# Sample rows read from PSUM, searches in eight steps, and fourteen lookups ahead at each unit's boundary in a two-layer attention and expert-retrieval kernel

## Chip, cores and metric

The kernel runs on one core of a Trainium2 chip. The metric is the device time of one execution in microseconds, the median of the runs. Everything is float32.

## What is computed

One step of a two-layer network over 384 tokens: 128 prompt tokens and 256 sample tokens, each of width 1024. Each layer has a dense half (modulated norm, one input projection, two kinds of attention and a short convolution, output projection) and then an expert retrieval, which takes most of the time here:

```python
q = (xc @ wq).reshape(128, 8, 2, 128)                  # 8 heads, 2 halves
sc = einsum('thcd,hcnd->thcn', q, sub_keys)            # 128 keys a half
s1, i1 = top_k(sc[:, :, 0], 16); s2, i2 = top_k(sc[:, :, 1], 16)
cand = s1[..., :, None] + s2[..., None, :]             # 256 pairs a head
top_s, pos = top_k(cand, 16)
eidx = (i1 * 128 + i2 of those pairs)                  # rows of two 16384-row tables
gate = softmax(top_s)
act = gelu(einsum('thkd,td->thk', take(u_tab, eidx), xc))
out = einsum('thk,thkd->td', gate * act, take(v_tab, eidx))
```

So each token reads 8 x 16 = 128 rows of 4 KB from the first table (U) and the same rows of the second (V), in each of two layers.

## The kernel before

**Units.** The 384 tokens are three tiles of 128, one token on each of 128 partitions. Tile 0 is the prompt, tiles 1 and 2 are the samples. A tile in a layer is called `tau` (0 to 5: prompt, sample, sample, and again for layer 1). Its 128 picks per token are two units of 64, so there are 12 units; unit `u` belongs to `tau = u // 2`. A lookup is one indirect DMA issued by GpSimd (L618): it takes one pick of all 128 tokens and brings 128 rows of 1024 floats into one of the 14 slots of `ring`. Each unit needs 64 U lookups and 64 V lookups, 1536 in all.

**What is done with a row.** For a U row VectorE computes the product with the token's own row and its sum (`dot`, L1381): in place in `ring`, with `h2[:, tau % 3, :]`, both in SBUF. After 64 of them `coefficients` (L1388 to L1397) makes the unit's factors, with a tanh on ScalarE. `turn` (L861, L862) transposes factors and picks on TensorE into `ps_acc`, ScalarE copies them (`copy_turned`, L1050 and L1051, and `spread`, L1069), and GpSimd makes `v_rows` of them (`take_unit`, L596). Only then can the unit's V lookups be issued. TensorE adds V rows in quads, four lookups at a time, with 16 matmuls (`add_rows`, L875), and frees four slots together. At the end of a `tau`, `copy_sum` (L1075) and `feed` (L1405 to L1409) bring the sum into `x`.

**Searches.** `route(n)` (L1329 to L1360) does the two-stage top 16 of one head for a tile on VectorE, some 30 instructions in a row. GpSimd's `take_head` (L588) waits for its picks before the head's first U lookup. Searches are made two heads ahead, in the middle of a head's 16 products.

**Segments.** Every engine walks the same list by hand. A segment has a unit `u` whose U rows are multiplied, a unit `v` (the one before) whose V rows are added, and sometimes dense work beside it:

```python
s0, p1, s1 = (0, S_TILES), (1, P_TILES), (1, S_TILES)
return (Segment(0, None, s0), Segment(1, 0, s0, True),
        Segment(2, 1), Segment(3, 2, p1), Segment(4, 3, p1), Segment(5, 4, p1), Segment(None, 5, p1, True),
        Segment(6, None, s1), Segment(7, 6, s1, True),
        Segment(8, 7), Segment(9, 8), Segment(10, 9), Segment(11, 10), Segment(None, 11))
```

`s0` and `s1` are the sample tiles' dense half in layers 0 and 1, `p1` the prompt's in layer 1; the prompt's in layer 0 comes first, alone. Segments with nothing beside them are called plain here: (2, 1), (8, 7), (9, 8), (10, 9), (11, 10), and the last. A segment has 64 items; at each item every engine first does its share of the dense work (`side.item()`), by a fixed weight, and then VectorE does `dot(i)`, and TensorE, at each fourth item, `add_rows` of V rows i-3 to i. The order in each engine's queue is fixed.

**Order of lookups.** `lookups()` writes GpSimd's order out. In a segment with both units the first `LEAD` = 6 places are U lookups only, then U and V alternate, and the last 6 are V lookups only; so seven U lookups stand ahead of V row 0. A lookup waits until the one 14 places before it has been used (`free_slot`), by VectorE for a U row and by TensorE for a V row.

**PSUM.** It has four tensors of 1024 columns: `ps_acc` for the sums, `ps_mb`, `ps_mm` and `ps_tr` for the dense work. Attention scores (`scores`, L754) alternate between the two halves of `ps_mm`, so that score `g` waits for exponential `g - 2`; transposed probabilities (`transpose_probs`, L765) alternate between the two halves of `ps_tr`. In a B head two score maps are made: VectorE takes the maxima of both (L1231, L1232), ScalarE the exponentials (L974), VectorE mixes them.

## Time and profile before

| | |
|---|---|
| median of 3 runs | 3205.22 us (3202.32 to 3216.55) |
| profiled execution: its own time | 3236.59 us |
| profiled execution: span in the profile | 3234.8 us |
| mean granted clock of TensorE | 0.684 of full speed |
| lookups | 805.40 MB of 963.27 MB moved |
| first U lookup of the segments (0,-), (1,0), (2,1), (3,2) | 269.7, 411.8, 807.2, 1003.0 us |
| of (4,3), (5,4), first V lookup of (-,5), then (6,-), (7,6) | 1212.8, 1478.6, 1704.2, 1796.6, 1925.3 us |
| of (8,7), (9,8), (10,9), (11,10), first V lookup of (-,11) | 2316.0, 2516.4, 2717.1, 2912.7, 3125.6 us |

Times are microseconds from the start of the span unless marked ns. PE is TensorE, DVE VectorE, ACT ScalarE, POOL GpSimd. A line of the timeline gives start, duration, engine, line of the kernel, operation and operands; in brackets stands how long the engine had been idle before it and what ended that. A name of a tensor can be that of another in the same memory (`h<-...` and `scores` are views).

### The profile page before, as it was taken

To read this page: it belongs to the slowest core of one execution; us is meant where nothing else is said; L and a number is where in the kernel's file an instruction comes from. 1 tells how busy PE (TensorE), PEld (TensorE's weight loads), DVE (VectorE), ACT (ScalarE), POOL (GpSimd) and SP (SyncE) were. 2 spreads that over 40 slices of the span, in tenths; PEclk is the share of its full clock that TensorE was granted. 3 is DMA by queue.
4 is the path that set the end of the run, shared out by engine and by line. 5 is a ranking of instruction groups with operands and counts; after the bars stand their busy time and mean duration, and the time that the engine had idled before them with its cause. 6 is when DMAs were issued, how large, how long until landed. Compare 5 with 4: busy or idle time off the path is not lost.

```text
span 3234.8 us, 22432 instructions
## 1 busy us (share of the span) xinstructions
PE 1552.9 (48%) x6476; PEld 676.8 (21%) x6476; DVE 1635.3 (51%) x3970; ACT 278.2 (9%) x730; POOL 1715.8 (53%) x1601
## 2 busy tenths in 40 slices
PE   6666668567234433333445747856423222232334
PEld 2343235244001110111222225424300000000001
DVE  1406676454656555455532596543556555565420
ACT  0211013011000000010000103210100000000000
POOL 0004511355677777436665660247577777777755
PEclk9778765788557666666678875677765656665567
DMA  8668962589998999658999890379799999998988
GB/s 298 247 237 281 353 220 85 208 319 341 361 332 319 379 380 368 241 198 301 340 375 368 312 359 26 125 268 360 258 333 335 326 337 346 345 349 316 339 313 311
DMA packets 299017, 963.27 MB, mean 298 GB/s; under 512 B 28280, under 2 KB 30712, under 8 KB 298128
## 3 DMA queue, kind: packets, MB, share of 16 engines
q0 software_dynamic: 221184, 805.40, 67.9%
q1 hardware_dynamic: 77712, 156.44, 13.4%
q8 instruction: 53, 0.87, 0.1%
q14 instruction: 68, 0.56, 0.0%
HBM read 959.12 MB, written 2.62 MB: 297 GB/s over the span
## 4 chain that ended last, share of the span: by engine, by line
issue 24%; PE 22%; POOL 19%; DMA 18%; DVE 14%; another core or an unknown queue 1%; ACT 1%; POOLq 0%; SPq 0%; DVEq 0%; ACTq 0%
POOL ring L618 19%; DMA ring<-peer_v,v_rows 11%; PE ps_acc L875 7%; DVE ring L1381 4%; PE ps_mm L700 3%; PE ps_mm L754 2%; PE ps_mm L813 2%; DMA weights<-ada_w 2%; DMA ring<-peer_u,u_rows 2%; PE ps_mm L841 1%; PE ps_mb L780 1%; DMA weights<-w_in 1%; DMA weights<-peer_wq 1%; PE ps_tr L765 1%
## 5 line engine op out<-in xcount | busy, mean ns | idle before, releaser
L875 PE MATMUL ps_acc<-ring,coef_cols 128*32 128x512 f32 x3072 | 629.5, 959 | 1327.4 <-DMA ring<-peer_v,v_rows 1310.7
L1381 DVE CUSTOM_DVE_ANT_0 ring<-ring,h 128x1024 f32<-128x1024 f32 x768 | 917.2, 1224 | 636.2 <-DMA ring<-peer_u,u_rows 611.5
L618 POOL DMA_INDIRECT ring<-peer_u,u_rows x768 | 842.4, 1097 | 635.8 <-DVE dots L1381 386.3
L618 POOL DMA_INDIRECT ring<-peer_v,v_rows x768 | 839.4, 1093 | 398.0 <-issue 217.3
L875 PEld LDWEIGHTS ps_acc<-ring,coef_cols 128*32 128x32 f32 x3072 | 124.2, 148 | 1756.8 <-issue 1755.6
L700 PE MATMUL ps_mm<-weights,hT 128*128 128x512 f32 x480 | 217.3, 612 | 30.1 <-DMA weights<-w_in 25.6
L841 PE MATMUL ps_mm<-hT,weights 128*128 128x128 f32 (+1 forms) x1024 | 201.3, 355 | 26.5 <-DMA weights<-peer_wq 21.4
L841 PEld LDWEIGHTS ps_mm<-hT,weights 128*128 128x128 f32 x1024 | 171.7, 213 | 92.1 <-issue 53.0
L588 POOL TENSOR_SCALAR u_rows<-picks 128x16 uint32<-128x16 f32 x48 | 23.6, 493 | 302.7 <-DVE picks L1360 301.7
L700 PEld LDWEIGHTS ps_mm<-weights,hT 128*128 128x128 f32 x480 | 92.9, 196 | 154.6 <-issue 117.3
L1405 DVE TENSOR_TENSOR h<-h,ps_acc 128x1024 f32<-128x1024 f32 x6 | 7.3, 1222 | 197.7 <-PE ps_acc L875 197.7
L813 PE MATMUL ps_mm<-weights,hT 128*128 128x512 f32 x192 | 95.8, 657 | 9.5 <-DMA weights<-w_out 6.2
L1231 DVE TENSOR_REDUCE rowmax<-ps_mm 128x1 f32<-128x384 f32 (+1 forms) x108 | 50.0, 463 | 91.4 <-PE ps_mm L754 79.3
L661 PE MATMUL ps_acc<-weights,condT 128*32 128x512 f32 x384 | 63.9, 798 | 66.6 <-DMA weights<-ada_w 66.6
L596 POOL TENSOR_SCALAR v_rows<-turned_rows 128x64 uint32<-128x64 f32 x12 | 8.3, 696 | 162.4 <-ACT turned L1051 162.4
L754 PE MATMUL ps_mm<-h,scores 32*128 32x384 f32 (+1 forms) x144 | 81.0, 849 | 23.8 <-ACT scores L974 20.2
L1069 ACT ACTIVATE coef_cols<-turned 64x16 f32<-64x16 f32 x96 | 21.9, 228 | 798.1 <-PE ps_acc L875 545.6
L1131 DVE TENSOR_TENSOR mods<-mods,ps_acc 128x512 f32<-128x512 f32 x24 | 16.5, 686 | 130.7 <-PE ps_acc L661 126.5
L1309 DVE TENSOR_TENSOR merged<-merged,ps_mb 128x512 f32<-128x512 f32 x12 | 8.2, 687 | 129.8 <-ACT merged L1004 129.8
L1381 DVE DVE_READ_ACCUMULATOR2_ANT dots<- 128x1 f32 x768 | 63.2, 82 | 0.0
L974 ACT ACTIVATE scores<-ps_mm,negmax 128x384 f32<-128x384 f32 (+1 forms) x108 | 54.3, 507 | 64.4 <-DVE negmax L1232 64.4
L1027 ACT ACTIVATE proj<-ps_mm 128x128 f32<-128x128 f32 (+1 forms) x64 | 21.1, 330 | 447.5 <-PE ps_mm L841 254.6
(182 smaller groups left out, 1539.3 us busy)
## 6 DMA issues: line engine op xcount, KB each, us to landing
weights<-ada_w SPq DMA_DIRECT2D x24, 2048.0 KB
weights<-w_in SPq DMA_DIRECT2D x20, 2048.0 KB
weights<-peer_wq SPq DMA_DIRECT2D x16, 2048.0 KB
weights<-w_out SPq DMA_DIRECT2D x8, 2048.0 KB
ring<-peer_u,u_rows POOLq DMA_INDIRECT x768
ring<-peer_v,v_rows POOLq DMA_INDIRECT x768
weights<-peer_keys SPq DMA_DIRECT2D x4, 1024.0 KB
par<-params SPq DMA_DIRECT2D x2, 1026.0 KB, 7.0
```

Of the source, the lines that this page charges most:

```text
L618: pool.indirect_dma_start(ring[:, place % RING, :], None, src, bass.IndirectOffsetOnAxis(ap=rows, axis=0)).then_inc(row_full[place % RING] ...
L661: last = pe.matmul(ps_acc[QROWS * j:QROWS * (j + 1), n % 2 * NB:(n % 2 + 1) * NB], condT[:, k, at:at + QROWS], w[:, k, :], start=(i == 0), ...
L700: last = pe.matmul(mm(i), hT[:, k, j * P:(j + 1) * P], w[:, k, :], start=(k == 0), stop=(k == KC - 1))
L754: pe.matmul(mm(g, nk * P), q, k, start=True, stop=True, tile_position=(lo, 0)).then_inc(score_mm, 1)
L765: last = pe.transpose(tr(head)[:, s * P:(s + 1) * P], w_.probs[:, probs_slot(head), s * P:(s + 1) * P], ident)
L780: last = pe.matmul(ps_mb[:, col:col + HD], w_.probsT[:, head % 2, s * P:(s + 1) * P], v, start=(s == 0), stop=(s == nk - 1))
L813: pe.matmul(mm(i), hT[:, k, j * P:(j + 1) * P], w[:, k, :], start=(k == 0), stop=(k == KC - 1))
L841: last = pe.matmul(mm(i, nt * P), w[:, k, (i % 4) * P:(i % 4 + 1) * P], hT[:, k, 0:nt * P], start=(k == 0), stop=(k == KC - 1))
L875: last = pe.matmul(ps_acc[QROWS * k:QROWS * (k + 1), b * NB:(b + 1) * NB], coef_cols[:, i // PART % 2, at:at + QROWS], ring[:, slot("v", n ...
L974: act.activation(w_.probs[:, probs_slot(head, second), 0:nk * P], mm(g, nk * P), ACT.Exp, bias=negmax[:, u:u + 1], scale=float(HD if u < A ...
L1231: step.after(dve.tensor_reduce(rowmax[:, u:u + 1], mm(j * UNITS + u, nk * P), AXX, ALU.max))
L1381: dve.tensor_tensor_reduce(row, row, h2[:, n // (2 * UNIT) % T, :], 1.0, 0.0, ALU.mult, ALU.add, dots[:, n // UNIT % 2, n % UNIT:n % UNIT ...
```

## The change

1. In the products of sample units (2 to 5 and 8 to 11, 512 of the 768) the token's row is read from `ps_tr`. A new ScalarE step, `hold_rows`, copies the 1024 columns of `h2` there, once for each of the four sample tiles and layers, when the tile before has all its products done; VectorE waits for it before the first product.
2. `ps_tr` is therefore taken while layer 1's prompt dense work (`p1`) runs beside units 3 to 5. For that work alone (`tight`) transposes go to `ps_mm` or a half of `ps_mb`, all scores to one half of `ps_mm` (score `g` waits for exponential `g - 1`), all transposed probabilities to the other half (one buffer in place of two), and TensorE transposes a head's probabilities before it makes the next scores.
3. `route` is a generator of eight steps; from the middle of a head on, one step is done before each product. Where a search's result is needed at once, it is run through whole, as before.
4. `LEAD` is 14: fifteen U lookups stand ahead of V row 0, and 14 V lookups alone end the segment. TensorE's `add_rows` and ScalarE's `spread` come `LAG` = 8 items later in segments with a U unit, and the last eight rows are added after the items.

```diff
-LEAD = 6
+LEAD = 14
+LAG = 8
+SAMPLES = [l * T + t for l in range(DEPTH) for t in S_TILES]
+        def tight(l, tiles):
+            return l > 0 and tiles == P_TILES
+        def scores_at(l, tiles, g, n):
+            return mm(0, n) if tight(l, tiles) else mm(g, n)
+        def probs_at(l, tiles, head, n):
+            return mm(1, n) if tight(l, tiles) else tr(head, n)
+        def buffers(l, tiles):
+            return 1 if tight(l, tiles) else 2
...
+                if l and tiles == S_TILES:
+                    pe.wait_ge(u_used, l * 2 * T * UNIT)
...
-                            if g >= 2:
-                                pe.wait_ge(exp_ready, nth(l, tiles, UNITS, g - 2))
+                            if g >= buffers(l, tiles):
+                                pe.wait_ge(exp_ready, nth(l, tiles, UNITS, g - buffers(l, tiles)))
...
-                        if head + 1 < HEADS:
+                        if head + 1 < HEADS and not tight(l, tiles):
                             scores(head + 1)
                         if head >= 1:
                             transpose_probs(head - 1)
+                        if head + 1 < HEADS and tight(l, tiles):
+                            scores(head + 1)
...
+                lag = 0 if g.u is None else LAG
...
-                    if g.v is not None and i % QUADS == QUADS - 1:
-                        add_rows(g.v, i - QUADS + 1)
+                    if g.v is not None and i % QUADS == QUADS - 1 and i >= lag:
+                        add_rows(g.v, i - lag - QUADS + 1)
+                for i in range(UNIT - lag if g.v is not None else UNIT, UNIT, QUADS):
+                    add_rows(g.v, i)
...
+            def hold_rows(tau):
+                act.wait_ge(u_used, 2 * tau * UNIT)
+                act.wait_ge(ps_ready, group_nth(tau // T, S_TILES, 15, 16))
+                act.wait_ge(h_ready, nth(tau // T, S_TILES, 2, 2 * len(S_TILES) - 1))
+                act.activation(ps_tr[:], h2[:, tau % T, :], ACT.Copy).then_inc(h_held, 1)
...
                 if g.u is not None:
                     gelu_tanh(g.u)
+                    if g.u % 2 and not g.last and (g.u + 1) // 2 in SAMPLES:
+                        hold_rows((g.u + 1) // 2)
...
                 if g.last:
                     side.end()
+                    if g.u is not None:
+                        hold_rows((g.u + 1) // 2)
...
-                dve.tensor_tensor_reduce(row, row, h2[:, n // (2 * UNIT) % T, :], 1.0, 0.0, ALU.mult, ALU.add,
+                tau = n // (2 * UNIT)
+                h = h2[:, 0, :]
+                if tau in SAMPLES:
+                    h = ps_tr[:]
+                    if n % (2 * UNIT) == 0:
+                        dve.wait_ge(h_held, held(tau))
+                dve.tensor_tensor_reduce(row, row, h, 1.0, 0.0, ALU.mult, ALU.add,
...
                     if i % TOPK == TOPK // 2 and head == routed and (head % P_HEADS or head // P_HEADS % T == 2):
-                        route(routed)
+                        for _ in routing:
+                            pass
+                        routing = route(routed)
                         routed += 1
+                    next(routing, None)
```

## Rows read from the trace of the kernel before

**Rows 1.** The page: GpSimd's busy tenths and the DMA engines' in 40 slices.

```profile
POOL 0004511355677777436665660247577777777755
DMA  8668962589998999658999890379799999998988
```

**Rows 2.** Windows, one for each stage or group of stages.

```profile
core 0: us, PE busy (x) PEld busy (x) DVE busy (x) ACT busy (x) POOL busy (x), PEclk, DMA share, GB/s
807.20:1003.00 195.80, 51.27 (x232) 9.99 (x236) 118.78 (x295) 1.42 (x6) 141.85 (x134) 0.56 0.94 348
2316.00:3112.20 796.20, 223.82 (x1006) 44.02 (x1006) 445.56 (x1042) 11.60 (x46) 579.81 (x531) 0.59 0.92 336
...
1003.00:1212.80 209.80, 88.61 (x346) 26.61 (x341) 117.85 (x280) 10.53 (x24) 145.60 (x134) 0.67 0.96 361
1212.80:1478.60 265.80, 92.16 (x398) 31.28 (x394) 138.53 (x370) 24.32 (x74) 137.60 (x133) 0.62 0.75 267
1478.60:1704.20 225.60, 109.82 (x554) 50.79 (x546) 102.69 (x211) 19.23 (x54) 139.70 (x133) 0.72 0.93 349
...
411.80:807.20 395.40, 267.08 (x1072) 158.16 (x1072) 214.86 (x534) 70.52 (x176) 137.32 (x133) 0.72 0.64 231
1925.30:2316.00 390.70, 257.56 (x1024) 156.63 (x1024) 206.72 (x519) 70.19 (x176) 140.85 (x133) 0.71 0.56 200
```

**Rows 3.** GpSimd's lookups: two groups from 2316 to 3112 us, then L618 from 3126.

```profile
L618 POOL DMA_INDIRECT ring<-peer_v,v_rows x256 | 284.4, 1111 | 116.8 <-issue 74.8 <-DVE dots L1381 24.6 <-remote 11.1
L618 POOL DMA_INDIRECT ring<-peer_u,u_rows x256 | 281.6, 1100 | 88.0 <-issue 74.4 <-PE ps_acc L875 7.3 <-POOL u_rows L588 6.4
...
L618 POOL DMA_INDIRECT ring<-peer_v,v_rows x64: 932/937/1022, 3125.6 to 3214.3; - x64
```

**Rows 4.** Timeline: lookups beside products (L1381) and beside L1405.

```profile
2500.10 1.99 POOL L618 DMA_INDIRECT ring<-peer_u,u_rows  x1 [0.30 <-issue]
...
2504.68 0.94 POOL L618 DMA_INDIRECT ring<-peer_u,u_rows  x1 [0.30 <-issue]
...
2510.68 1.23 DVE L1381 CUSTOM_DVE_ANT_0 ring<-ring,h 128x1024 f32<-128x1024 f32 x1 [3.42 <-DMA ring<-peer_u,u_rows]
...
2522.16 1.22 DVE L1405 TENSOR_TENSOR h<-h,ps_acc 128x1024 f32<-128x1024 f32 x1 [8.81 <-PE ps_acc L875]
2522.70 0.94 POOL L618 DMA_INDIRECT ring<-peer_u,u_rows  x1 [0.31 <-issue]
```

**Rows 5.** GpSimd's waits: the span, then 2316 to 3112 us (total, times, longest).

```profile
POOL ring L618 <- DVE dots L1381: 459.0, 81, 19.0
...
POOL ring L618 <- PE ps_acc L875: 10.9, 15, 1.9
```

**Rows 6.** Timeline of GpSimd at boundaries between segments.

```profile
2514.26 0.94 POOL L618 DMA_INDIRECT ring<-peer_v,v_rows  x1 [0.30 <-issue]
...
2531.43 1.02 POOL L618 DMA_INDIRECT ring<-peer_v,v_rows  x1 [0.91 <-POOL v_rows L596]
...
1494.45 1.00 POOL L596 TENSOR_SCALAR v_rows<-turned_rows 128x64 uint32<-128x64 f32 x1 [7.37 <-ACT turned L1051]
...
2020.50 0.37 POOL L596 TENSOR_SCALAR v_rows<-turned_rows 128x64 uint32<-128x64 f32 x1 [55.61 <-ACT turned L1051]
...
2314.88 0.25 POOL L588 TENSOR_SCALAR u_rows<-picks 128x16 uint32<-128x16 f32 x1 [18.66 <-DVE picks L1360]
```

**Rows 7.** Timeline inside the attention of layer 1's prompt tokens.

```profile
1367.09 3.60 PE L875 MATMUL ps_acc<-ring,coef_cols 128*32 128x512 f32 x16 [11.18 <-DMA ring<-peer_v,v_rows]
...
1371.66 0.37 ACT L974 ACTIVATE scores<-ps_mm,negmax 128x128 f32<-128x128 f32 x1
...
1371.98 0.49 DVE L1329 MAX8 half_top<-scores 128x8 f32<-128x128 f32 x2
...
1372.17 0.87 PE L754 MATMUL ps_mm<-scores,h 32*128 32x128 f32 x4 [0.63 <-ACT scores L974]
...
1381.33 0.19 DVE L1360 SCALAR_TENSOR_TENSOR picks<-pair_key 128x32 f32<-128x32 f32 x1
...
1383.48 1.14 POOL L618 DMA_INDIRECT ring<-peer_u,u_rows  x1 [18.96 <-DVE dots L1381]
```

More of the change, by code:

```diff
@@ L679, in norm @@
                     for k in range(KC):
-                        last = pe.transpose(ps_tr[:, k * P:(k + 1) * P], src[:, k * P:(k + 1) * P], ident)
+                        last = pe.transpose(transposed(l, tiles)[:, k * P:(k + 1) * P], src[:, k * P:(k + 1) * P], ident)
                     last.then_inc(h_mm, 1)
@@ L799, in dense_stages @@
                     for k in range(KC):
-                        last = pe.transpose(ps_tr[:, k * P:(k + 1) * P], merged[:, k * P:(k + 1) * P], ident)
+                        last = pe.transpose(transposed(l, tiles)[:, k * P:(k + 1) * P], merged[:, k * P:(k + 1) * P], ident)
                     last.then_inc(mergedT_mm, 1)
@@ L1084, in _ @@
                     side = start_beside(of, modulate, dense_stages)
+                lag = 0 if g.u is None else LAG
                 if g.v is not None:
```

68 lines of the change are left out of this document (44 added, 24 removed).

## Prediction

> **What bounds the kernel now.** I read the page first: its busy lines, then its slices over time, to see which engine could be the limit [rows 1]. None is: GpSimd is busy 53% of the span, TensorE and VectorE no more. The DMA line is at 8 or 9 tenths in most slices and falls to 0 to 3 around two places, near 450 us and near 1970 us. So I cut the span into the kernel's own stages, by the first lookup of each unit in the timeline [rows 2]. Three kinds show. In the five plain stages, where only lookups, products and sums run, the DMA engines are busy 92 to 94% at 336 to 348 GB/s. Beside layer 1's prompt tokens it is 96%, 75%, 93%. In the two stages beside sample tokens it is 64% and 56%: there the order of the dense work sets the time, not the lookups.
>
> Next, what a lookup costs. A lookup is one GpSimd instruction and 128 rows of 4 KB, 0.524 MB. Alone it takes 0.94 us and the next follows 0.30 us behind, so 1.24 us [rows 3]. In the four plain stages from 2316 to 3112 us the 512 lookups take 1.11 and 1.10 us each, 0.17 above 0.94: 512 x 0.17 = 86 us of GpSimd time. The timeline says when: a lookup issued while products (L1381, two operands in SBUF) run back to back takes 1.99 us, it ends with a product; one that runs across L1405, the same length but with one operand in PSUM, takes 0.94 [rows 4].
>
> The last stretch has lookups of V alone and no products: 64 of them from 3125.6 to 3214.3 us, 88.7 / 63 = 1.41 us each, all of 0.94 us [rows 3]. So with GpSimd free the transfers themselves set the pace. The best mixed stage, at 1003 us, moves 361 GB/s [rows 2]; 0.524 MB at 361 GB/s is 1.45 us.
>
> Last, who makes GpSimd wait [rows 5]: over the span VectorE's products (slots of the ring not yet free), 459 us in 81 waits. In the four plain stages TensorE's additions, which hold the V slots, make it wait only 11 us.
>
> **The change part by part.**
>
> (a) *Products from PSUM.* The 512 products of units 2 to 5 and 8 to 11 read `ps_tr` in place of `h2`. By the L1405 pair they take as long and no longer hold GpSimd [rows 4]. A lookup there goes back to 1.24 us, which is under the 1.45 of the transfers, so the transfers become the limit. Now the five plain stages take 195.8 + 796.2 (four of them) = 992 us for 640 lookups, 1.55 each [rows 2].
>
> (b) *Fourteen lookups ahead.* At an even V unit the chain is: last V lookup 2514.26, sums, L1405, turn, `v_rows`, first V lookup 2531.43. That is 17.2 us [rows 6]. Seven U lookups, 8.7 us, stand in it now; the next V row comes fifteen U lookups on, 15 x 1.24 = 18.6 us, so the rest of the chain is covered, at the transfers' pace amply. What could be late next is U row 14, which needs the slot of product 0; it comes behind `feed`, whose three 1.2 us steps begin with L1405 at 2522.2 [rows 4], with the gate between them: about 2529, before the slot is wanted at 2534. The v-only tail grows from 6 to 14 lookups. VectorE has no product in it; it is busy 119 of 196 us [rows 2], so this has cover in plain stages.
>
> So a plain stage is 128 lookups at a pace r plus about 1.2 us for `take_unit`. From below r is 1.41, the V stretch; from above 1.53, which the stage at 807 does already (195.8 / 128). A second limit: the first V slot of a quad is wanted again 8 lookups after the quad's last lookup starts; that takes about 6.0 us until it is used (issued 2504.68, product at 2510.68 [rows 4]) and 3.6 us of L875 [rows 7], with TensorE's granted clock at 0.56 to 0.59 in these stages, mostly its lower level, 1.2 GHz [rows 2], 10 us with the semaphores, or 1.25 us a lookup, and 1.4 to 1.45 when a landing is 1 to 1.5 us late. I take 1.45, nearer the V stretch since its rate has been seen in a mixed stage too. 640 x 1.45 + 6 = 934: **58 us less**; the bounds give 84 and 7.
>
> The Trainium skill (DMA: Bandwidth & Descriptors, "Where 436 GB/s comes from") puts the HBM side at about 358 GB/s for one core, which would speak against any large gain: 0.524 MB / 358 = 1.46 us, an estimate, and the same five stages at 943 us, 49 less. The stage at 1003 moves 361, so the trace agrees within 1%.
>
> (c) *Searches in eight steps.* Each of VectorE's searches (L1329 to L1360) is 9.5 us without a product between, as from 1371.98 to 1381.5, and GpSimd's wait of 18.96 us ends behind it [rows 7]. Between products the steps are 1 to 3 us, and two lookups take 2.5 us, so most of a search is then under the issue of lookups. In plain stages it is in (a)'s pace. In the two sample stages and at the prompt's attention the engines wait for each other in turn; I count 5 us for each sample stage (0 to 12) and 6 for the prompt stage.
>
> (d) *Prompt attention of layer 1 in one score buffer.* This adds waits. The second map of a B head (6 of them) may only be scored after the first one's exponential: the exponential starts at 1371.66 and the score that waits for it at 1372.17, 0.5 us; the score takes up to 0.5, and two semaphores 0.4, so 1.4 us in which VectorE waits in order and the products behind it too [rows 7]. Each of 12 heads has its transpose ahead of its score, 0.4 us and the copy's signal: 12 x 0.5. Together 14 us, bounds 0 (other waits cover it; TensorE comes 11.2 us late with the quad before anyway) and 40 (each map, 18, waits 2.2 us).
>
> (e) *The stages beside layer 1's prompt.* At 1003 us the DMA engines are busy 96%: 4 us. At 1212 (75%): -14 from (d), +6 from (c), +2 for the turned rows, +6 of the GpSimd time above 0.94: no change. At 1478 (93%): the wait of 7.4 us for `v_rows` and 0.9 behind it [rows 6] go, and some of the product waits: 10 us. Sum **14 us less**, bounds 45 less and 35 more.
>
> (f) *Sample stages at 411 and 1925.* GpSimd waits 55.6 us for `v_rows` with seven U rows landed [rows 6]. It looks like the prize of (b), but VectorE is then in the attention with one or two heads' steps at every product (VectorE busy 207 of 391 us [rows 2], the rest mostly in waits for two engines that wait for it), so rows landed earlier wait in the ring. The sums run 8 items later (`LAG`), as V rows come 8 later: no change there. The tail of 14 V lookups falls into the wait for the first searches, 18.7 us up to 2314.9 [rows 6]: 8 x 1.41 = 11 us each is covered; without that cover it is 22 us more. **10 us less** by (c).
>
> (g) *`hold_rows`.* Four copies of 1,024 columns into PSUM, which before does not have; by the nearest row, L1405 [rows 4], 1.2 us each, from 1 to 2. Two lie behind whole searches, two are seen: **2 us more**.
>
> Sum: 58 + 14 + 10 - 2 = **80 us less** of 3236.6, the profiled execution's own time (1.8 us around its span); that is 1% above the median of the runs. 3156.6 / 3236.6 x 3205.2 = **3126 us**.
>
> **The rivals.**
> - *The ring sets the pace.* V slots wait for TensorE in quads at its lower clock, and GpSimd gives back as waits on L875 what it no longer loses. For: 1.25 to 1.45 us a lookup is as near as the transfers. Against: only 11 us of such waits in four plain stages. At 1.50 the stages save 26, with (e), (f) halved 35 in all: 3170 us.
> - *The single score buffer makes it slower.* If each of the 12 heads held VectorE until TensorE's next quad (11.2 us for its V rows, 3.6 us of sums, 1.5 of dense work: 16 us [rows 7]) in place of every second or third, seven more such rounds would be 112 us: 3156.6 + 112, scaled 3237 us. It decides from 80 / 12 = 6.7 us a head on. Against: both programs keep their order by items, so a head cannot slip past one.
> - *The dense stages gain.* If the waits of 459 us [rows 5] come mostly from whole searches and the ring, with 14 rows ahead, feeds VectorE through the attention, 30 us for each sample stage and 20 beside the prompt in place of 5 and 14: 58 + 60 + 20 - 2 = 136 us less, 3070 us.
> - *PSUM does not free GpSimd*: the other operand and the output stay in SBUF, and lookups stay at 1.1 us. The L1405 row speaks against it. Left are the boundaries and searches, 35 us: 3170 us.
> - *The longer tail is not covered* at the ends of the sample stages, 22 us: 3148 us.
>
> **How the numbers follow.** Forecast 50% (own range 3090 to 3160), ring 22%, slower attention 7%, dense gain 12%, PSUM no help 6%, tail 3%. The range for 8 in 10 leaves out most of the slower case and the far ends of the dense gain and the ring: 3065 to 3190. This kernel can be told from no change at about 0.5%, 16 us. Faster by more: 0.50 + 0.12 + 0.03 and most of 0.22 and 0.06, 0.86. Within: 0.07. Slower: 0.07.
>
> **What would show it.** The 512 lookups of the sample units at a mean of 0.94 to 0.97 us; plain stages of 184 to 190 us with the DMA engines at 96% or more; no wait over 2 us before a first V lookup in them; GpSimd's waits on L875's successor up from 11 us in the four plain stages to 20 to 40; the stage of the prompt's attention within 15 us of 265.8; the sample stages within 10 us of 395 and 391. Wrong it would be if plain stages stay above 193 us, or if the sample stages or the attention move by more than 20 us either way.

## Result, and the profile after

The changed kernel takes 3008.5 us (3001.5 to 3011.0, 4 runs), the kernel before beside it 3203.8 us: ratio 0.938, 95% interval 0.935 to 0.941. The forecast was 3126 us with a range down to 3065, so the gain is 195 us where 79 were expected.

The page of the changed kernel, the two lines that answer to [rows 1]: GpSimd's busy tenths and the DMA engines'.

```profile
POOL 0002531256677666535565664126667767776665
...
DMA  8677992389999999858998986248989999999988
```

Its windows, by the same stages as [rows 2], each from a unit's first lookup to the next unit's (us, busy time of each engine, granted clock, DMA share, GB/s).

```profile
783.60:957.90 174.30, 53.94 (x242) 10.30 (x234) 116.99 (x295) 4.92 (x15) 122.38 (x133) 0.54 1.02 397
2202.30:2906.70 704.40, 226.02 (x1040) 45.19 (x1040) 435.76 (x1042) 15.72 (x58) 490.37 (x532) 0.61 0.99 382
957.90:1154.50 196.60, 87.87 (x342) 26.25 (x342) 115.79 (x280) 11.46 (x25) 123.72 (x133) 0.71 0.99 381
1154.50:1404.40 249.90, 97.48 (x386) 35.37 (x386) 138.45 (x370) 24.29 (x74) 123.12 (x134) 0.61 0.78 286
1404.40:1622.80 218.40, 110.11 (x556) 50.89 (x557) 101.71 (x211) 18.82 (x52) 123.11 (x133) 0.73 0.94 361
416.40:783.60 367.20, 262.90 (x1042) 160.60 (x1046) 214.44 (x535) 68.03 (x168) 143.48 (x134) 0.72 0.65 236
1835.20:2202.30 367.10, 259.30 (x1024) 159.55 (x1024) 211.28 (x530) 70.91 (x175) 143.74 (x133) 0.71 0.60 215
```

GpSimd's groups in the four plain stages from 2202 us, which answer to the first two of [rows 3], and its waits there (total, times, longest).

```profile
L654 POOL DMA_INDIRECT ring<-peer_u,u_rows x256 | 243.8, 952 | 92.2 <-issue 62.5 <-DVE dots L1448 15.1 <-POOL u_rows L624 10.9
L654 POOL DMA_INDIRECT ring<-peer_v,v_rows x257 | 241.5, 940 | 109.2 <-issue 77.6 <-PE ps_acc L915 21.0 <-DVE dots L1448 8.9
```

```profile
POOL ring L654 <- PE ps_acc L915: 24.7, 27, 1.9
POOL ring L654 <- DVE dots L1448: 24.0, 47, 1.7
POOL v_rows L632 <- ACT turned L1094: 13.0, 1, 13.0
```

The last stretch, with V lookups alone (duration min/median/max, first and last start), answers to the last of [rows 3]; the timeline at two boundaries answers to [rows 6].

```profile
L654 POOL DMA_INDIRECT ring<-peer_v,v_rows x64: 933/937/1022, 2906.7 to 2985.1; - x64
```

```profile
520.95 0.39 POOL L632 TENSOR_SCALAR v_rows<-turned_rows 128x64 uint32<-128x64 f32 x1
...
2392.30 0.40 POOL L632 TENSOR_SCALAR v_rows<-turned_rows 128x64 uint32<-128x64 f32 x1
2393.60 1.02 POOL L654 DMA_INDIRECT ring<-peer_v,v_rows  x1 [0.91 <-DVE dots L1448]
```

What the reader is to see. The lookups cost 0.95 and 0.94 us in place of 1.10 and 1.11. The first V lookup after a boundary no longer waits for its rows where U lookups stand ahead of it; 55.6 us of such a wait stood in the sample stage. At the two boundaries where none do, the starts of (-,5) and (-,11), 16.3 and 13.0 us are left. The waits on TensorE's sums in the four plain stages rose from 11 to 24.7 us, inside the 20 to 40 forecast. The plain stages move 382 to 397 GB/s. And the last stretch, whose instructions the change doesn't touch, now goes at (2985.1 - 2906.7) / 63 = 1.24 us a lookup, not 1.41. That last row is the one that doesn't fit the forecast, and nothing in the diff explains it. The plain stages, 174.3 + 704.4 less the single wait of 13.0, make 865.7 where the prediction's 992, which ends 1.3 us earlier at that boundary, should have become 934.

### The profile page after: what moved, and what is told of

Same layout as the page of the kernel before. It is cut to its first block, busy times and chain, and to the rows that moved or that the text cites. A ratio compares the mean times of both kernels' runs of the same rounds, so it can differ in the third digit from the quotient of the medians.

```text
span 3009.1 us, 22486 instructions
## 1 busy us (share of the span) xinstructions
PE 1559.4 (52%) x6476; PEld 688.4 (23%) x6476; DVE 1619.8 (54%) x3970; ACT 282.1 (9%) x734; POOL 1558.1 (52%) x1601
## 4 chain that ended last, share of the span: by engine, by line
DMA 26%; PE 25%; issue 17%; DVE 17%; POOL 13%; ACT 1%; POOLq 0%; SPq 0%; DVEq 0%; ACTq 0%
DMA ring<-peer_v,v_rows 17%; POOL ring L654 13%; PE ps_acc L915 8%; DVE ring L1448 7%; DMA ring<-peer_u,u_rows 4%; PE ps_mm L738 3%; PE ps_mm L792 3%; PE ps_mm L853 2%; PE ps_mm L881 2%; PE ps_mb L818 1%; DMA weights<-w_in 1%; DMA weights<-peer_wq 1%; PE ps_tr L803 1%; DMA weights<-ada_w 1%; PE ps_mb L677 1%
## 5 line engine op out<-in xcount | busy, mean ns | idle before, releaser
L915 PE MATMUL ps_acc<-ring,coef_cols 128*32 128x512 f32 x3072 | 611.4, 937 | 1125.6 <-DMA ring<-peer_v,v_rows 1125.6
L654 POOL DMA_INDIRECT ring<-peer_u,u_rows x768 | 786.4, 1024 | 682.8 <-DVE dots L1448 466.1
L654 POOL DMA_INDIRECT ring<-peer_v,v_rows x768 | 747.4, 973 | 425.4 <-issue 225.6
L1448 DVE CUSTOM_DVE_ANT_0 ring<-ring,ps_tr 128x1024 f32<-128x1024 f32 x512 | 618.1, 1220 | 371.4 <-DMA ring<-peer_u,u_rows 354.4
L1448 DVE CUSTOM_DVE_ANT_0 ring<-ring,h 128x1024 f32<-128x1024 f32 x256 | 307.8, 1223 | 109.8 <-DMA ring<-peer_u,u_rows 95.7
L738 PE MATMUL ps_mm<-weights,hT 128*128 128x512 f32 x480 | 223.0, 625 | 25.8 <-DMA weights<-w_in 21.2
L853 PE MATMUL ps_mm<-weights,hT 128*128 128x512 f32 x192 | 98.5, 672 | 9.5 <-DMA weights<-w_out 6.1
```

The source lines that it names most:

```text
L654: pool.indirect_dma_start(ring[:, place % RING, :], None, src, bass.IndirectOffsetOnAxis(ap=rows, axis=0)).then_inc(row_full[place % RING] ...
L738: last = pe.matmul(mm(i), hT[:, k, j * P:(j + 1) * P], w[:, k, :], start=(k == 0), stop=(k == KC - 1))
L853: pe.matmul(mm(i), hT[:, k, j * P:(j + 1) * P], w[:, k, :], start=(k == 0), stop=(k == KC - 1))
L915: last = pe.matmul(ps_acc[QROWS * k:QROWS * (k + 1), b * NB:(b + 1) * NB], coef_cols[:, i // PART % 2, at:at + QROWS], ring[:, slot("v", n ...
L1448: dve.tensor_tensor_reduce(row, row, h, 1.0, 0.0, ALU.mult, ALU.add, dots[:, n // UNIT % 2, n % UNIT:n % UNIT + 1]).then_inc(u_used, 1)
```

## Experiments

**The parts, one at a time and one left out.** Each is the changed kernel with parts undone, by these edits:

```diff
 products from PSUM and single buffers undone:
-            return l > 0 and tiles == P_TILES
+            return False
-                h = h2[:, 0, :]
-                if tau in SAMPLES:
-                    h = ps_tr[:]
+                h = h2[:, tau % T, :]
 (and VectorE's wait for h_held, the two uses of hold_rows, TensorE's wait for u_used)
 searches in steps undone:
-                        routing = route(routed)
+                        for _ in route(routed):
+                            pass
-                    next(routing, None)
 lead undone:
-LEAD = 14
-LAG = 8
+LEAD = 6
+LAG = 0
```

Psum_only, split_only and lead_only keep one part; no_psum, no_split and no_lead leave one out; before_again is the kernel before and after_again the changed one, once more.

> The kernel before with part 1 and 2 alone: sample rows in ps_tr, prompt attention of layer 1 in single buffers; six lookups ahead, no lag, searches whole. Theory A (GpSimd's stretched lookups set the pace of the plain stages, and the transfers can go at about 1.35 us a lookup, not 1.45): the five plain stages fall from 992 us to 900 to 920, the boundary waits before V row 0 stay at 6 to 9 us, sample stages stay at 395 and 391; total 80 to 120 us less than before. Theory B (a longer queue of lookups does it): plain stages fall by 40 us at most, total 50 us less or under.

> The kernel before with the searches in eight steps alone. Theory A: the waits of GpSimd behind a whole search shrink by 6 to 9 us each where the dense work is, 10 to 30 us in all; plain stages at most 5 us less each. Theory B, that whole searches drain the ring in plain stages too: 8 to 12 us less in each plain stage, 50 us or more in all.

> The kernel before with fourteen lookups ahead and the lag of eight alone. Theory A: the waits before V row 0 at even units go (25 to 30 us over the plain stages and those beside the prompt), lookups beside products still take 1.10 us; the sample stages gain 10 to 20 us each; total 40 to 70 us less. Theory B: plain stages fall to 1.40 us a lookup or less with lookups still at 1.10 us; total 100 us less or more.

> The kernel before once more, for a second profile. The last stretch of V lookups alone took 1.41 us a lookup in the first profile (issue gaps of 3.8 us behind late landings) and 1.24 after the change, with the same instructions. Theory A: that stretch was slowed in that one execution by something outside the kernel, and goes at 1.24 to 1.36 here. Rival: it is the kernel's own, 1.41 again.

> The changed kernel once more, beside the kernel before on this chip. In its first profile the last stretch of V lookups went at 1.24 us a lookup and the plain stages at 1.35, where four other kernels of this family and the kernel before show 1.41 in the last stretch with the same instructions. Theory A (the parts together do it, the pace is the kernel's own): 1.24 again in the last stretch and a ratio of 0.94 again. Theory C (the pace of the transfers belongs to the chip or to that load of the tables): 1.41 again here, and a ratio of 0.955 to 0.965, near the sum of the single parts.

> The changed kernel with products from SBUF (parts 3 and 4 alone, no single buffers). Additive theory: 0.981 x 0.997 = 0.978 of before. Theory of a joint effect: whole searches and late V rows had covered each other, 0.965 or less.

> The changed kernel with searches whole (parts 1, 2 and 4). Additive: 0.989 x 0.997 = 0.986 of before. Joint effect: 0.975 or less, plain stages under 970 us.

> The changed kernel with six lookups ahead and no lag (parts 1, 2 and 3). Additive: 0.989 x 0.981 = 0.970 of before. Joint effect of PSUM and steps: the two together free GpSimd and keep products even, plain stages at 1.42 us a lookup or less (910 us), 0.960 of before; the boundary waits of 6 to 13 us stay.

Measured, the first four rows on chip 11 of the machine, the other four on chip 10, the ratios to the kernel before on the same chip (3249.7 us, 13 runs, and 3264.7 us, 7 runs), with the lengths of stages read from the profiled executions (plain: five stages; prompt attention: the stage at 1212 us of before; sample: the two stages beside sample tokens; last: us a lookup in the last stretch):

| kernel | us | ratio | 95% | plain | prompt attention | sample | last |
|---|---|---|---|---|---|---|---|
| before_again | 3260.1 | one run | | 1013.2 | 269.0 | 789.4 | 1.41 |
| psum_only | 3213.2 | 0.989 | 0.984 to 0.995 | 978.9 | 268.3 | 784.7 | 1.41 |
| split_only | 3190.2 | 0.981 | 0.976 to 0.986 | 986.9 | 253.2 | 761.4 | 1.41 |
| lead_only | 3236.2 | 0.997 | 0.994 to 1.000 | 1011.0 | 264.4 | 770.2 | 1.41 |
| no_psum | 3188.0 | 0.976 | 0.971 to 0.980 | 989.2 | 256.9 | 740.8 | 1.42 |
| no_split | 3192.9 | 0.979 | 0.975 to 0.983 | 966.1 | 263.5 | 772.1 | 1.42 |
| no_lead | 3179.5 | 0.974 | 0.970 to 0.979 | 977.6 | 259.7 | 760.0 | 1.42 |
| after_again | 3130.4 | 0.959 | 0.955 to 0.963 | 949.7 | 253.4 | 745.4 | 1.42 |

Three things follow. The split searches, priced at 16 us in the prediction, are the largest single part, about 60 us, and most of it lies beside dense work: 28 us of the sample stages, 16 of the prompt's attention, 26 in the plain stages. The lead alone is worth almost nothing in the plain stages and 19 us in the sample stages, where the prediction gave it none. And the parts don't simply add. Over the whole kernel the single ratios multiply to 0.968 where all together give 0.959, a difference about as large as the intervals. The lead is clearer: alone it gives 13 us (3249.7 to 3236.2), taken out of the changed kernel it costs 49 (3130.4 to 3179.5), and in the plain stages 2 and 28.

Of the expectations, before_again's theory A fell: its last stretch took 1.41 us a lookup again. Psum_only's 900 to 920 us of plain stages failed: it was 978.9, with 37 us less in all and not 80 to 120. Lead_only stayed under both of its theories (40 to 70 us, and 100). Split_only gained the 50 us and more of its theory B, but in the plain stages only 5 us each, as theory A had it. No_psum and no_split came out at or a little below their sums of parts (0.976 for 0.978, 0.979 for 0.986), no_lead above it (0.974 for 0.970); none reached the ratio of the joint effect expected of it, though no_split's plain stages, 966.1 us, are under the 970 of that theory.

The table also shows that chips 10 and 11 gave other conditions than the first measurement. The kernel before took 3250 to 3265 us, the changed one 3130 and not 3008, and the last stretch kept its mean of 1.41 to 1.42 us in every kernel. So the ratio isn't one number.

**The pair once more.** Before_third and after_third are the two kernels unedited, on chip 7.

> The kernel before once more, for a profile taken on the same chip as the runs beside it. If the chip's transfers are quick (its last stretch of second-table lookups near 1.25 us each, where the first profile had 1.41), theory 'transfers' expects the kernel before still at 1.50 to 1.56 us a lookup in its plain stages, since GpSimd's issue holds it there, and about 3200 us; if they are slow, 1.41 and about 3260 us.

> The changed kernel once more, on the same chip as the kernel before. Theory 'transfers': 0.938 of the kernel before if the last stretch goes at 1.25 us a lookup, 0.959 if it goes at 1.41. Rival: the ratio is one number, near 0.95, and the two measurements so far scatter about it.

Measured: 3263.3 us for the kernel before (one run; 3259.5 over its other runs) and 3126.7 for the changed one, ratio 0.960 (0.956 to 0.965); last stretches at 1.42 us in both. By theory "transfers" this is what a chip with a last stretch of 1.41 gives. Windows of before_third, then of after_third: the stage at 816 (786), the four plain ones, the prompt's attention, the two sample stages.

```profile
816.30:1015.60 199.30, 50.96 (x232) 10.05 (x236) 118.49 (x295) 1.43 (x6) 146.50 (x133) 0.59 0.93 342
2337.80:3151.20 813.40, 236.45 (x1040) 46.43 (x1040) 445.38 (x1042) 14.26 (x54) 576.52 (x533) 0.57 0.91 331
1223.70:1491.70 268.00, 94.00 (x394) 32.28 (x390) 138.39 (x370) 24.35 (x74) 138.77 (x133) 0.61 0.74 264
419.30:816.30 397.00, 268.54 (x1072) 159.46 (x1072) 214.83 (x535) 70.40 (x176) 137.33 (x134) 0.70 0.62 225
1949.30:2337.80 388.50, 254.85 (x1024) 157.05 (x1024) 209.22 (x526) 70.61 (x176) 136.34 (x133) 0.72 0.56 204
```

```profile
786.30:973.00 186.70, 54.38 (x250) 10.46 (x246) 116.69 (x295) 4.91 (x15) 123.08 (x134) 0.57 0.97 371
2241.10:3008.30 767.20, 230.37 (x1042) 45.89 (x1042) 436.74 (x1042) 18.35 (x64) 492.77 (x532) 0.59 0.94 351
...
1178.80:1433.10 254.30, 98.01 (x386) 35.95 (x382) 138.02 (x370) 24.26 (x74) 122.59 (x133) 0.61 0.77 277
...
414.60:786.30 371.70, 265.55 (x1042) 160.90 (x1046) 214.37 (x534) 67.83 (x168) 142.56 (x133) 0.72 0.64 232
1875.60:2241.10 365.50, 259.80 (x1022) 159.96 (x1022) 211.06 (x530) 68.00 (x169) 143.50 (x133) 0.72 0.60 216
```

The sample stages of the two measurements of the changed kernel are nearly alike (371.7 and 365.5 against 367.2 and 367.1), and VectorE's and TensorE's busy times too. What differs is the plain stages, 953.9 against 878.7 us, the DMA rate in them, 351 against 382 GB/s, and 20 us beside the prompt (684.7 against 664.9).

The mean of the last stretch hides two things. The timeline of after_third there:

```profile
3047.11 3.64 PE L915 MATMUL ps_acc<-ring,coef_cols 128*32 128x512 f32 x16 [4.00 <-DMA ring<-peer_v,v_rows]
...
3058.03 0.93 POOL L654 DMA_INDIRECT ring<-peer_v,v_rows  x1 [3.94 <-remote]
...
3058.43 2.46 PE L915 MATMUL ps_acc<-ring,coef_cols 128*32 128x512 f32 x16 [2.56 <-DMA ring<-peer_v,v_rows]
3059.27 0.93 POOL L654 DMA_INDIRECT ring<-peer_v,v_rows  x1 [0.30 <-issue]
```

A lookup is 0.93 + 0.30 us, and after the 18th, 34th and 50th of this stretch GpSimd stands 2.5 to 3.9 us for a slot (and 1.9 after the 14th). Fifteen steps of 1.24 and one of 4.87 are 23.5 us, the period seen. Three such stalls, 3.8 us each, stand in the first profile of the kernel before, and they are in all twelve profiles from chips 7, 10 and 11; the first profile of the changed kernel and the six from chips 0 and 8 (below) have none. For the first measurement no chip is on record. "A chip with the stalls" means below one of the three, on which the kernel before took 3250 to 3265 us and not 3200.

What holds GpSimd there isn't told by the profile, which writes `remote` for a wait whose end it can't name. It isn't plainly a late row: the slot wanted at 3058.03 was that of the 21st lookup, whose sums begin at 3047.11 and take 3.64 us, so by these rows it was used up 3.3 us before GpSimd fell idle. Such waits aren't confined to the last stretch. In the four plain stages the waits of this kind are (total, times, longest), in before_third, after_third and psum_only:

```profile
POOL ring L618 <- remote: 21.7, 8, 3.3
...
POOL ring L654 <- remote: 58.9, 20, 4.0
...
POOL ring L654 <- remote: 72.8, 22, 3.8
```

No profile without the stalls has one anywhere. So of the 62.8 us by which these four stages are longer in after_third than in the changed kernel's first profile (767.2 and 704.4), 58.9 are such waits; and psum_only, whose lookups take 0.95 us as in the changed kernel, loses 72.8 us to them. The kernel before, whose lookups are stretched, meets fewer.

Where there are no stalls, the rows themselves come nearly as slowly as GpSimd issues them. In the changed kernel's first profile TensorE starts on four new rows every 5.12 us in most of the last stretch, 1.28 us a lookup, with the DMA engines at 1.03:

```profile
2942.52 1.92 PE L915 MATMUL ps_acc<-ring,coef_cols 128*32 128x512 f32 x16 [1.80 <-DMA ring<-peer_v,v_rows]
2947.64 3.32 PE L915 MATMUL ps_acc<-ring,coef_cols 128*32 128x512 f32 x16 [3.20 <-DMA ring<-peer_v,v_rows]
...
2918.00:2984.00 66.00, 34.01 (x204) 7.43 (x196) 0.00 (x0) 0.91 (x4) 49.83 (x54) 0.82 1.03 410
```

**Shorter rows.** What stretches a lookup beside a product with two operands in SBUF [rows 4] is called the port here, and the lock in some of the expectations. If the rate of transfers holds the changed kernel and the port holds the kernel before, fewer bytes should help the one and not the other. The edit, in either kernel (SHORT is 896, in the half kernels 512; the ring is set to zero at the start; the indexed view must be contiguous, so other rows are fetched and the results are not those of the network):

```diff
+            def short(table):
+                n = table.shape[0] * table.shape[1] // SHORT
+                flat = table.rearrange("n d -> (n d)")
+                return flat[0:n * SHORT].rearrange("(n d) -> n d", d=SHORT)
-                pool.indirect_dma_start(ring[:, place % RING, :], None, src,
+                pool.indirect_dma_start(ring[:, place % RING, 0:SHORT], None, short(src),
```

> The kernel before, with each lookup bringing 896 consecutive values for each partition in place of 1024 (the last 128 columns of every ring slot stay zero, the products and sums still run over 1024 columns, so the output is of other rows). Theory 'transfers': the kernel before is held mostly by GpSimd's issue (about 1.55 us a lookup in the plain stages, transfers 1.41), so an eighth less to transfer gives it only some 60 us, ratio to the kernel before about 0.98; the last first-table-free stretch goes from 1.41 us a lookup to the issue rate, 1.24. Rival 'something else differed between the two chips': transfers are not what held either kernel, and this one falls by under 0.5 per cent.

> The changed kernel, with each lookup bringing 896 consecutive values for each partition in place of 1024 (the last 128 columns of every ring slot stay zero, so the output is of other rows). Theory 'transfers': with the lock gone its pace is that of the transfers, so it gains about twice what the kernel before gains from the same cut: near 3010 us where the changed kernel takes 3130, ratio to the kernel before about 0.923, and to the shortened kernel before about 0.94, the ratio of the first measurement. Rival 'something else': it stays above 3100 us, and its ratio to the shortened kernel before stays at 0.96.

> The kernel before with PSUM products alone (lead, lag and searches as before), with each lookup bringing 896 consecutive values for each partition in place of 1024 (the last 128 columns of each ring slot stay zero, so the output is of other rows). Theory 'transfers': what the shorter lookup saves can only be had where the lock is gone. With transfers out of the way the PSUM products take about 0.2 us from each of 640 lookups of the plain stages and some from the rest, so the ratio to the kernel before falls from the 0.989 of full rows to about 0.96. Rival 'scheduling': the searches and the lead set the pace beside it, and the ratio stays above 0.98.

> The kernel before with the searches in eight steps alone, with each lookup bringing 896 consecutive values for each partition in place of 1024 (the last 128 columns of each ring slot stay zero, so the output is of other rows). Theory 'transfers': the lock is still there, so GpSimd holds the pace at about 1.5 us a lookup, and the ratio to the kernel before is that of full rows, 0.981, within half a per cent. Rival: the split gains from quicker transfers too, 0.97 or less.

> The kernel before, with each lookup bringing 512 consecutive values for each partition in place of 1024 (the other columns of each ring slot stay zero, the products and sums still run over 1024, so the output is of other rows). Theory 'stalls': on a chip whose last stretch of second-table lookups has a mean of 1.42 us, that is 1.25 us for each lookup and a stall of 3.8 us after every sixteenth, and an eighth fewer bytes left it so; if bytes have no part in it, half the bytes leave it too, and the kernel is within 1 per cent of the kernel before with rows an eighth shorter (0.98 of the kernel before on such a chip, 1.00 on one without the stalls). Theory 'bytes': half the bytes remove the stalls, the last stretch goes at 1.25 us on any chip. In both, GpSimd's issue and its waits for the port keep the plain stages of this kernel above 1.5 us a lookup.

> The changed kernel with the same cut to 512 values. Theory 'stalls': with the lock gone its floor is the issue of a lookup, 1.25 us, which no cut in bytes lowers, so on a chip without the stalls it stays near the 2951 us of rows an eighth shorter, 0.92 of the kernel before, and on one with them it keeps its distance, 0.94. Theory 'bytes': it goes below 2900 us, under 0.91, on either chip.

| kernel | us | ratio | 95% | plain | last |
|---|---|---|---|---|---|
| before_short | 3202.1 | 1.001 | 0.999 to 1.004 | 1004.9 | 1.25 |
| after_short | 2950.5 | 0.922 | 0.918 to 0.926 | 858.2 | 1.25 |
| psum_short | 3202.7 | 0.983 | 0.978 to 0.989 | 982.7 | 1.42 |
| split_short | 3190.2 | 0.980 | 0.975 to 0.985 | 1010.8 | 1.42 |
| before_half | 3149.3 | 0.985 | 0.980 to 0.990 | 1011.8 | 1.25 |
| after_half | 2866.5 | 0.895 | 0.891 to 0.900 | 840.9 | 1.25 |

The ratios are to the kernel before with full rows on the same chip: 3198.8 us for the first two (chip 0), 3259.5 for the next two (chip 7), 3201.5 for the last two (chip 8). So psum_short and split_short ran on a chip with the stalls, the other four on one without them.

Before_half's windows (its two pieces of plain stages), and its lookups in the second piece:

```profile
788.10:987.50 199.40, 53.17 (x240) 10.29 (x240) 118.66 (x295) 1.42 (x6) 157.30 (x134) 0.56 0.61 178
2232.00:3044.40 812.40, 228.13 (x1040) 45.48 (x1040) 445.85 (x1042) 14.23 (x54) 629.77 (x533) 0.58 0.59 166
```

```profile
L627 POOL DMA_INDIRECT ring<-peer_v,v_rows x256 | 338.5, 1322 | 80.4 <-issue 75.5 <-POOL v_rows L600 3.6 <-PE ps_acc L884 0.9
L627 POOL DMA_INDIRECT ring<-peer_u,u_rows x256 | 282.9, 1105 | 87.6 <-issue 67.9 <-POOL u_rows L592 10.9 <-PE ps_acc L884 8.8
```

After_half, the same two views:

```profile
767.10:933.80 166.70, 54.46 (x262) 10.78 (x258) 115.84 (x295) 4.91 (x15) 124.27 (x133) 0.56 0.73 221
2097.60:2771.80 674.20, 222.43 (x1040) 44.76 (x1040) 435.85 (x1042) 16.48 (x61) 497.13 (x533) 0.62 0.69 200
```

```profile
L663 POOL DMA_INDIRECT ring<-peer_u,u_rows x256 | 246.9, 964 | 87.9 <-issue 59.1 <-DVE dots L1457 17.9 <-POOL u_rows L628 8.2
L663 POOL DMA_INDIRECT ring<-peer_v,v_rows x257 | 245.1, 954 | 82.4 <-issue 67.8 <-PE ps_acc L924 8.5 <-DVE dots L1457 5.1
```

This pair settles what holds the plain stages of each kernel. With half the bytes and the DMA engines at 0.59, the kernel before needs 1011.8 us for them. With full rows it needs 1005.3 and 1012.7 on chips with the stalls; on one without, the nearest profile is that of single_only (below), which is the kernel before but for the prompt's attention in layer 1: 982.4 us, with lookups of 1.15 and 1.08 us.

```profile
818.10:1011.00 192.90, 51.95 (x232) 10.02 (x236) 118.84 (x295) 1.43 (x6) 145.85 (x133) 0.54 0.95 354
2316.50:3106.00 789.50, 233.38 (x1040) 45.73 (x1040) 445.30 (x1042) 14.26 (x54) 585.04 (x533) 0.58 0.93 341
```

Fewer bytes don't make these stages shorter, so there GpSimd is the limit. It waits 0.3 us in all for products in the four later stages of before_half, but its lookups rose to 1.32 and 1.11 us: slots that come free sooner let lookups start beside more products, and the port takes back all that the transfer gave, and more. The changed kernel falls to 840.9, 1.31 us a lookup, nearly GpSimd's issue of 1.25. Its full rows cost 879 on a chip without the stalls and 950 to 954 on one with them. Outside the plain stages both kernels gain from half the bytes: beside the prompt 61 us of the changed kernel (664.9 to 604.1) and 38 of the kernel before (700.9 in single_only to 663.0), which is why before_half has a ratio under 1.

Two theories of mine fell here. "Transfers" in its first form, bytes by rate, expected before_short at 0.98 and psum_short at 0.96; they were 1.001 and 0.983, the second with 982.7 us of plain stages, as with full rows, 978.9. Its last stretch shows why: still 1.42, with the same stalls.

```profile
3120.39 3.81 PE L924 MATMUL ps_acc<-ring,coef_cols 128*32 128x512 f32 x16 [3.55 <-DMA ring<-peer_v,v_rows]
...
3121.59 0.94 POOL L663 DMA_INDIRECT ring<-peer_v,v_rows  x1 [3.84 <-remote]
```

Stalls of 3.84 us are no matter of an eighth of the bytes. "Stalls", that bytes have no part at all, expected after_half near 2951 us and before_half within 1% of before_short; they were 2867 and 1.6% less. Whether half the bytes would remove the stalls wasn't tried, as chip 8 has none. So both count: bytes cost the changed kernel 142 us between full and half rows without the stalls (3008.5 to 2866.5, measured apart), 38 of them in the plain stages; the stalls cost some 120 more (3128 against 3008).

**The single score buffer.** Of the PSUM part only the single buffers of the prompt's attention, in the kernel before: products from `h2`, searches whole, lead 6.

```diff
-                h = h2[:, 0, :]
-                if tau in SAMPLES:
-                    h = ps_tr[:]
+                h = h2[:, tau % T, :]
-LEAD = 14
-LAG = 8
+LEAD = 6
+LAG = 0
```

> The kernel before with one edit: in layer 1 the prompt tile's attention has a single buffer for scores and one for transposed probabilities, and its transposes go to other banks; products, searches and lead are as before. The prediction priced this at 14 us in the stage of the prompt's attention (265.8 us before), which gives a ratio of 1.004. Rival, from the stage of the kernel with PSUM products alone (268.3 against 269.0): the single buffer costs nothing, the stage stays within 3 us and the ratio is 1.000.

Measured 3206.8 against 3198.8 us, ratio 1.003 (1.001 to 1.005): 8 us, between the two. The window of the stage:

```profile
1218.20:1490.10 271.90, 98.75 (x398) 34.97 (x394) 139.08 (x370) 24.40 (x74) 140.49 (x133) 0.60 0.74 261
```

It stands beside 265.8, 269.0 and 268.0 in three profiles of the kernel before, all with the stalls, and 266.1 in before_short on the same chip: 3 to 6 us more, not 14.

**Ten ahead in place of fourteen.**

```diff
-LEAD = 14
-LAG = 8
+LEAD = 10
+LAG = 4
```

> The changed kernel with 10 first-table lookups ahead at a boundary and the sums 4 lookups behind, in place of 14 and 8. If the gap ahead of a unit's first second-table lookup (57 us with six ahead, 5 us with fourteen) is what the lead is worth, it comes back in part (some 25 us at each of four places) and the time lies half way between the kernel with six ahead (0.974) and the changed one (0.959): 0.967. Rival: eight more lookups ahead were more than needed, four do as well, 0.959; then the deferred sums cost nothing or something.

Measured 3020.9 us, ratio 0.944 (0.941 to 0.948); the changed kernel has 0.938 (0.935 to 0.941) in the first measurement, both without the stalls. `v_rows` waits 33.7 us in the sample stage, where six ahead give 55.6 and fourteen none:

```profile
515.15 0.37 POOL L632 TENSOR_SCALAR v_rows<-turned_rows 128x64 uint32<-128x64 f32 x1 [33.66 <-ACT turned L1094]
```

```profile
416.30:793.40 377.10, 267.53 (x1060) 161.73 (x1056) 214.71 (x535) 71.34 (x177) 143.95 (x134) 0.72 0.64 232
1842.30:2219.20 376.90, 257.11 (x1024) 158.46 (x1024) 211.45 (x530) 71.35 (x177) 146.15 (x133) 0.72 0.58 209
793.40:965.90 172.50, 50.49 (x232) 9.97 (x236) 116.67 (x295) 1.42 (x6) 122.93 (x133) 0.58 1.01 394
2219.20:2917.40 698.20, 228.51 (x1040) 45.18 (x1040) 437.31 (x1042) 15.15 (x55) 490.45 (x532) 0.60 0.99 386
```

Each sample stage is 10 us longer than with fourteen, the plain stages are not (870.7 against 878.7). So the last four steps of the lead are worth 20 us, in the sample stages alone; over the whole kernel 12 us are left of it (3020.9 against 3008.5, measured apart), in the middle between the two expectations, that half of the lead's worth comes back and that nothing does. No version with the full rows beat the changed kernel.

## Why the prediction was off

The direction was right, the size was not: 195 us in place of 79 against the first pair, 133 to 134 against the second. By the prediction's steps: the first pair's profile of before has the stalls and that of after has not, so its differences hold both; the second pair is of one chip, with stalls; the last column sets the changed kernel's first profile beside single_only's, both without.

| step | forecast | first pair | second pair | without stalls |
|---|---|---|---|---|
| (a), (b) plain stages, without the last wait for `v_rows` | -58 | 992 to 865.7, -126 | 1000 to 943, -57 | 970.4 to 865.7, -105 |
| (e) with (c), (d): beside the prompt | -14 | 701.2 to 664.9, -36 | 706.1 to 684.7, -21 | 700.9 to 664.9, -36 |
| (f) sample stages | -10 | 786.1 to 734.3, -52 | 785.5 to 737.2, -48 | 783.9 to 734.3, -50 |
| the short stretches with one table | 0 | -17 | -12 | -9 |

The last column adds up to 200 us, the difference of the two spans (3209.1 and 3009.1 us); single_only is itself 8 us slower than the kernel before. By the prediction's own signs it was wrong too: each sample stage moved by 23 to 28 us, over the 20 allowed, and plain stages of 174 to 176 us are under the 184 to 190 forecast.

**Right: PSUM frees GpSimd, and transfers then limit.** The lookups' mean of 0.94 to 0.95 us was inside the 0.94 to 0.97 given, the DMA engines were at 0.99 (though half the bytes save only 38 us of 879 here, as GpSimd's issue of 1.24 us is close behind), the boundaries went (0.91 us of waiting at 2393.6), and the waits on the sums came out as said. On the chip with the stalls even the size came out, (943 - 6) / 640 = 1.46 us a lookup, forecast 1.45, but by luck: 58.9 us of that time are waits that the prediction didn't know, not transfers.

**The step that failed first: the lower bound of r.** The prediction took 1.41 us, the mean of the last stretch, as the pace of the transfers, and so no case of it could go below. That mean was 1.24 us of issue and three stalls of 3.8 us. Without the stalls r came to (865.7 - 6) / 640 = 1.34. A lower floor stood in the prediction's own trace, in TensorE's steps on four rows: between longer ones there are steps of 5.12 us, 1.28 us a lookup, the same step that the changed kernel's stretch keeps without the stalls.

```profile
3147.03 1.92 PE L875 MATMUL ps_acc<-ring,coef_cols 128*32 128x512 f32 x16 [1.55 <-issue]
...
3152.15 3.57 PE L875 MATMUL ps_acc<-ring,coef_cols 128*32 128x512 f32 x16 [3.20 <-DMA ring<-peer_v,v_rows]
```

One trace could not tell that other executions lack the stalls, though it had a hint: the profiled execution took 3236.6 us and the runs beside it 3202 to 3217, and the prediction scaled by that 1% where the pace had to change. A lower bound of 1.28 gives 640 x 1.28 + 6 = 825 us for the plain stages and would have kept 865.7 within it. In (d) the two semaphores' 0.4 us, and in (b) what they add to the 9.6 us of the second limit, stand in no row; the score in [rows 7] starts 0.14 us after the exponential's end.

The Trainium skill (DMA: Bandwidth & Descriptors, "Where 436 GB/s comes from") gives the HBM side about 358 GB/s for one core, and the prediction found the trace in agreement. The changed kernel's plain stages moved 382 and 397 GB/s, so the measurement goes beyond that figure here; the estimate of 943 us that was made from it meets the 943 of the chip with the stalls by coincidence, and is 77 too many without them. The Trainium skill's HBM Reference ("Specifications (TRN2)") says what the prediction passed over: 358 is the share with both cores of a pair streaming, and a core alone measures well above it. The 397 GB/s agree with that; whether a neighbour's traffic makes the stalls, no run here shows.

**Mis-sized: the sample stages.** (f) gave the lead nothing there, arguing that V rows landed earlier would wait in the ring, and (c) gave the searches 5 us a stage. Alone, the split searches are 28 us and the lead 19 in the two stages, together with the rest 44 to 52. A 9.5 us search stood in VectorE's order between dense steps for which TensorE and ScalarE wait, as I read it; no wait of theirs was read before and after. The lead closed a wait of 55.6 us in which GpSimd did nothing. This is the rival "the dense stages gain", to which the prediction gave 12% and 30 us a stage: it was 23 to 28. That rival was the mechanism beside the forecast's, not in place of it, and both happened.

**Mis-sized: the single score buffer.** 14 us were forecast, 3 to 8 measured, and 16 us of the split searches in the same stage outweighed it: 265.8 became 249.9.

**Not seen: the parts need each other.** The prediction summed the parts. In the plain stages, on the chips with the stalls, the lead gives 2 us alone and 28 with the other two in place; PSUM and the split searches give 34 and 26 alone but 36 together (no_lead, 977.6 us). The sum of the three alone, 62, happens to equal the whole, 63. What each part is worth without the stalls wasn't measured: psum_only, whose remaining time holds 72.8 us of them in four stages, could be worth more there.

**Open.** What the stalls are. They come after every sixteenth lookup of the last stretch, which is also every 23.5 us; sixteen rows are also one part of the coefficients (`PART`) in the kernel, and which of these they go by wasn't tried. Whether they belong to a chip or to the hour is open too: the profiles of one chip agree with one another, but each chip was used at one time only. Nor is there a profile of the unedited kernel before without them; single_only, 1.53 us a lookup in its plain stages (982.4 / 640), stands in for it.

## What to carry to other kernels

Before a mean is taken as the floor of a resource, look at the single steps behind it, and at the engine that uses the result as well as at the one that asks for it: a mean of 1.41 us was an issue of 1.24 with a stall in every sixteenth step, rows came every 1.28 us at best, and the floor decides how low the range must reach. A kernel held by an engine's instruction stream doesn't show how quick the transfers can be; the gain from freeing that engine is then as uncertain as the transfers, and halving the bytes in both kernels tells which of them hangs on what. A long serial piece on an engine that alternates with two others costs time there: the searches in steps gave 28 us in the two sample stages, and 26 in the five plain ones, where the prediction had taken them as covered.

## What the runs showed of the hardware

- A lookup's duration depended on what VectorE did and not on its bytes: 0.94 to 0.95 us with 4 KB rows and 0.95 to 0.96 with 2 KB where the products read PSUM, but a mean of 1.08 to 1.15 with 4 KB rows and up to 1.32 with 2 KB beside products with both operands in SBUF.
- The last stretch ran at 1.24 to 1.25 us a lookup in seven profiles (chips 0 and 8, and the changed kernel's first) and at 1.41 to 1.42 in thirteen (chips 7, 10 and 11, and the first of the kernel before), with stalls of 2.5 to 3.9 us after every sixteenth; an eighth fewer bytes left the stalls as they were. The kernel before differed by 2% between the two (3200 and 3260 us), the changed kernel by 4% (3008.5 and 3128).
- Waits of GpSimd whose end the profile can't name, up to 4 us, stand throughout the profiles with the stalls (20 in four stages of after_third) and in none of the others.
- With products from PSUM, gathered rows of 4 KB moved at 382 to 397 GB/s over whole stages, and at 410 in a stretch without products (2918 to 2984 us of the changed kernel's first profile).
